# Six layer norms of a two-block transformer kernel: shift by the mean of the first chunks, sum squares while the last chunks come

## The reference

```python
def layer_norm(x, g, b):
    xf = x.astype(jnp.float32)
    mu = jnp.mean(xf, axis=-1, keepdims=True)
    var = jnp.mean(jnp.square(xf - mu), axis=-1, keepdims=True)
    return ((xf - mu) * lax.rsqrt(var + LN_EPS) * g + b).astype(x.dtype)

for l in range(DEPTH):                                   # DEPTH = 2
    h = layer_norm(ALPHA * h + 0.5 * swiglu(h, ffn1_w_up[l], ffn1_w_down[l]), ln_g[l, 0], ln_b[l, 0])
    mix = hybrid_mixer(h, ...)                           # its last product is with w_o
    h = layer_norm(ALPHA * h + mix, ln_g[l, 1], ln_b[l, 1])
    h = layer_norm(ALPHA * h + 0.5 * swiglu(h, ffn2_w_up[l], ffn2_w_down[l]), ln_g[l, 2], ln_b[l, 2])
```

## Time and profile before

| | before |
|---|---|
| median of 3 runs | 2914.3 us (2912.72 to 2917.24) |
| the profiled execution, its own time | 2911.84 us |
| its span in the trace | 2909.9 us |
| TensorE busy | 2790.0 us, 96% of the span |
| VectorE busy | 1999.8 us, 69% |
| ScalarE busy | 1681.8 us, 58% |
| GpSimd busy | 637.7 us, 22% |
| mean granted TensorE clock | 0.979 |

### The profile page before, as it was taken

One profiled execution on the slowest core, in us unless ns is written; L12 is line 12 of the kernel. 1 busy time (PEld: TensorE's weight loads), 2 busy tenths in 40 slices (PEclk: granted clock), 3 DMA queues, 4 the chain that ended last, 5 costly groups with the idle time before them and its releaser, 6 DMA issues.

```text
span 2909.9 us, 67986 instructions
## 1 busy us (share of the span) xinstructions
PE 2790.0 (96%) x27848; PEld 2301.9 (79%) x27848; DVE 1999.8 (69%) x1916; ACT 1681.8 (58%) x1776; POOL 637.7 (22%) x489
## 2 busy tenths in 40 slices
PE   9999989989999899799989999989999999999998
PEld 7877768878877688597878888779788797797884
DVE  4556565555565645566755465768899999999986
ACT  5435655455356454445655445636777777777775
POOL 3304012111031121002012002013242242332432
PEclk9999999999999999899999999989999999999999
DMA  8664357666633566463466754448999999999996
GB/s 231 172 186 134 93 161 198 172 170 178 199 116 106 162 175 175 126 190 121 150 167 190 216 161 134 127 157 308 382 391 378 393 384 379 395 379 382 393 381 235
DMA packets 657500, 665.40 MB, mean 229 GB/s; under 512 B 25302, under 2 KB 513116, under 8 KB 657276
## 3 DMA queue, kind: packets, MB, share of 16 engines
q1 hardware_dynamic: 655696, 659.75, 69.1%
q0 software_dynamic: 704, 0.59, 0.3%
q10 hardware_dynamic: 876, 1.79, 0.2%
HBM read 661.01 MB, written 1.05 MB: 228 GB/s over the span
## 4 chain that ended last, share of the span: by engine, by line
PE 89%; DVE 4%; ACT 2%; issue 2%; DVEq 1%; POOL 0%; DMA 0%; POOLq 0%; ACTq 0%; SPq 0%
PE ps L1793 22%; PE ps L1795 22%; PE ps L1794 22%; PE ps L2414 3%; PE ps L2413 3%; PE ps L2415 3%; PE ps L1834 1%; PE ps L1835 1%; PE ps L1840 1%; PE ps L1934 1%; DVE w_lo L1115 1%; PE ps L2046 1%; PE ps L1940 1%; PE ps L2066 1%; PE ps L2370 1%
## 5 line engine op out<-in xcount | busy, mean ns | idle before, releaser
L1793 PE MATMUL ps<-x_hi,w_hi 128*128 128x128 f16 (+2 forms) x5440 | 1232.6, 250 | 15.0 <-DVE prod L1130 7.3
L1795 PE MATMUL ps<-x_hi,w_lo 128*128 128x128 f16 (+2 forms) x5440 | 1232.3, 250 | 0.0
L1794 PE MATMUL ps<-x_lo,w_hi 128*128 128x128 f16 (+2 forms) x5440 | 1232.1, 250 | 0.0
L1115 DVE SCALAR_TENSOR_TENSOR w_lo<-w,w_hi 128x2048 f16<-128x2048 f32 (+4 forms) x338 | 689.7, 2051 | 323.6 <-ACT w_hi L659 319.4
L659 ACT ACTIVATE w_hi<-w 128x2048 f16<-128x2048 f32 (+4 forms) x338 | 563.8, 1673 | 182.8 <-PE ps L1795 157.9
L1793 PEld LDWEIGHTS ps<-x_hi,w_hi 128*128 128x128 f16 x5440 | 533.9, 98 | 74.0 <-issue 14.6
L1794 PEld LDWEIGHTS ps<-x_lo,w_hi 128*128 128x128 f16 x5440 | 533.9, 98 | 49.4
L1795 PEld LDWEIGHTS ps<-x_hi,w_lo 128*128 128x128 f16 x5440 | 533.7, 98 | 46.2
L1535 DVE SCALAR_TENSOR_TENSOR w_lo<-w,w_hi 128x2048 f16<-128x2048 f32 x224 | 544.8, 2456 | 31.2 <-ACT w_hi L1045 31.2
L1045 ACT ACTIVATE w_hi<-w 128x2048 f16<-128x2048 f32 x224 | 419.1, 1904 | 43.0 <-DMA w<-in_moe_w_down 21.3
L1775 POOL CAST ff<-pb 128x512 f16<-128x512 f32 x56 | 140.2, 2503 | 634.3 <-DVE pb L1616 634.3
(11 more groups left out here) (346 smaller groups left out, 4270.6 us busy)
## 6 DMA issues: line engine op xcount, KB each, us to landing
w<-in_ffn_w_up SPq DMA_DIRECT2D x176, 512.0 KB, 5.1
w<-in_moe_w_gate SPq DMA_DIRECT2D x80, 1024.0 KB, 9.0
w<-in_moe_w_up SPq DMA_DIRECT2D x80, 1024.0 KB, 9.2
w<-in_moe_w_down SPq DMA_DIRECT2D x64, 1024.0 KB, 8.2
w<-in_w_in SPq DMA_DIRECT2D x112, 512.0 KB, 4.7
mix<-in_moe_w_down SPq DMA_DIRECT2D x48, 1024.0 KB, 8.5
w<-in_mix_w_in SPq DMA_DIRECT2D x64, 512.0 KB, 4.9
mix<-in_moe_w_gate SPq DMA_DIRECT2D x32, 1024.0 KB, 9.6
```

Of the source, the lines that this page charges most:

```text
L1115: vec.scalar_tensor_tensor(k.w_lo[:, s, 0:size], k.w32[:, s, 0:size], WS, k.w_hi[:, s, 0:size], ALU.mult, ALU.subtract).then_inc(k.parts_r ...
L1793: pe.matmul(acc, w_hi, x_hi, start=first, stop=False)
L1794: pe.matmul(acc, w_hi, x_lo, start=False, stop=False)
L1795: return pe.matmul(acc, w_lo, x_hi, start=False, stop=last)
```

## The change

All six norms are made over. The constant matrix gets a companion `first_w` whose entries average over the first 6 chunks (down) or the first 4 (`wo`).

- **Shift.** When the first 6 (4) chunks are in, TensorE makes their mean (`shift`), behind unit 12 of a down phase or in the middle of unit 2 of `wo`. VectorE (`center`) subtracts it from these chunks, and prepares the others as `h*WS*ALPHA - shift`, so that the last products are only added to them.
- **Squares.** ScalarE squares the first chunks right away. GpSimd adds the squares up in float32 (`add_squares`: 6 additions for chunks 0 to 6 in a down phase, 3 for chunks 0 to 3 in `wo`), with a drain after each. TensorE takes that sum with one product (in a down phase ahead of unit 15, the last), and the rest of the squares behind the last unit.
- **What is left of the mean.** Only the unsummed chunks are multiplied with `mean_w` (the shifted first ones have sum zero). VectorE copies this rest out of PSUM, squares it, and subtracts the square from the mean of squares. GpSimd takes the rest off all 8 chunks (`take_off`), and VectorE scales each chunk once that is done for it.
- **Order on ScalarE.** The splits of the next phase's units 2 and 3 now stand around the 8 writes of `h`: unit 2 ahead of them, unit 3 behind them. The steps of the next phase that made them leave them out.
- **Clock.** 13 products of `mean_w` with itself (`keep_warm`) behind each norm's last sum; 30 in place of 18 at the start.
- The down phases and `wo` are written out in place of loops, and `wo` on VectorE gets an order by hand.

```diff
-WARM_UP = 18
+WARM_UP = 30
+KEEP_WARM = 13
+EARLY_DOWN, EARLY_WO = 6, 4
+SHIFT_STEP, SQUARES_STEP, SUMS_STEP = 2 * EARLY_DOWN, 2 * EARLY_DOWN + 1, 2 * KC - 2
...
 # ScalarE
+    def early_squares(n, early):
+        for c in range(early):
+            act.wait_ge(k.ln_centered, centered_before(n) + c + 1)
+            square(c)
+    def down_norm(n, phase, q, vec0, between=None):
+        def take(trip, j, g, q):
+            u = trip * SLOTS + j
+            if u == SHIFT_STEP and between is not None:
+                between()
+            if u == SQUARES_STEP:
+                early_squares(n, EARLY_DOWN)
+            if u > SQUARES_STEP:
+                c = EARLY_DOWN + u - SQUARES_STEP - 1
+                if c == KC - 1:
+                    root_ready()
+                act.wait_ge(k.vec_evac, vec0 + phase.base + 2 + c + 1)
+                square(c)
+        over_units_ahead(act, phase, q, split, take, loop=False)
-    def layer_norm(n, b0):
-        root_ready()
-        for c in range(KC):
-            act.wait_ge(k.ln_centered, n * KC + (c + 1))
-            act.activation(k.sq[:, c, :], k.h[:, c, :], ACT.Square).then_inc(k.ln_squared, 1)
-        act.wait_ge(k.ln_var, n + 1)
-        act.activation(k.std[:, 0, :], k.ps[:, 5, 0:T1], ACT.Sqrt, bias=k.eps[:, 0:1]).then_inc(k.ln_std, 1)
+    def layer_norm(n, b0, q, following):
+        act.wait_ge(k.ln_spread, n + 1)
+        act.activation(k.std[:, 0, :], k.tmp[:, 1, :], ACT.Sqrt, bias=k.eps[:, 0:1]).then_inc(k.ln_std, 1)
         for c in range(KC):
             act.wait_ge(k.ln_scaled, n * KC + (c + 1))
             act.activation(k.x_hi[:, c, :], k.sq[:, c, :], ACT.Identity, bias=k.col[:, b0 + c:b0 + c + 1]).then_inc(k.x_hi_ready, 1)
+        split(following + 2, q, UNIT)
         for c in range(KC):
             a = act.activation(k.h[:, c, :], k.sq[:, c, :], ACT.Identity, bias=k.col[:, b0 + c:b0 + c + 1])
         a.then_inc(k.h_ready, 1)
+        split(following + 3, q, UNIT)
...
 # VectorE
-    def add_sum(m):
-        vec.tensor_tensor(k.tmp[:, 2:3, :], k.tmp[:, 2:3, :], k.h[:, bass.ds(m, 1), :], ALU.add).then_inc(k.sum_added, 1)
-        vec.drain()
+    def center(n, early):
+        shift = k.ps[:, 4, 0:T1]
+        vec.wait_ge(k.ln_mean, n + 1)
+        for c in range(early):
+            vec.tensor_tensor(k.h[:, c, :], k.h[:, c, :], shift, ALU.subtract).then_inc(k.ln_centered, 1)
+        for c in range(early, KC):
+            vec.scalar_tensor_tensor(k.h[:, c, :], k.h[:, c, :], WS * ALPHA, shift, ALU.mult, ALU.subtract)
         vec.drain()
+    def down_norm(n, phase, q):
+        def take(trip, j, g, q):
+            u = trip * SLOTS + j
+            if u == SHIFT_STEP:
+                center(n, EARLY_DOWN)
+            if u % 2 == 0:
+                return
+            m, acc = u // 2, k.ps[:, 2 * (j // 2), 0:T1]
+            unit_used(g, q)
+            if m < EARLY_DOWN:
+                vec.scalar_tensor_tensor(k.h[:, m, :], k.h[:, m, :], WS * ALPHA, acc, ALU.mult, ALU.add).then_inc(k.vec_evac, 1)
+                a = add_first(m)
+                if m == EARLY_DOWN - 1:
+                    a.then_inc(k.first_summed, 1)
+            else:
+                vec.tensor_tensor(k.h[:, m, :], k.h[:, m, :], acc, ALU.add).then_inc(k.vec_evac, 1)
+        over_units_ahead(vec, phase, q, split, take, loop=False)
+    def wo_norm(n, q):
+        split(g + 2, q, UNIT)
+        split(g + 3, q, UNIT)
...
+        add_pair(0, True)
+        add_first(1)
+        add_pair(1, True)
+        add_first(2)
+        add_first(3).then_inc(k.first_summed, 1)
+        split(g + 4, q, UNIT)
+        center(n, EARLY_WO)
+        add_pair(2, False)
+        vec.wait_ge(k.wo_half, n // 3 + 1)
+        vec.tensor_tensor(k.h[:, 6, :], k.h[:, 6, :], k.ps[:, 2, 0:T1], ALU.add).then_inc(k.wo_half_out, 1)
+        split(g + 5, q, UNIT)
+        unit_used(g + 3, q)
+        vec.tensor_tensor(k.h[:, 7, :], k.h[:, 7, :], k.ps[:, 3, 0:T1], ALU.add).then_inc(k.vec_evac, 1)
     def layer_norm(n, g0, b0):
-        vec.wait_ge(k.ln_mean, n + 1)
-        for c in range(KC):
-            vec.tensor_tensor(k.h[:, c, :], k.h[:, c, :], k.ps[:, 4, 0:T1], ALU.subtract).then_inc(k.ln_centered, 1)
+        vec.wait_ge(k.ln_rest, n + 1)
+        vec.tensor_copy(k.tmp[:, 0, :], k.ps[:, 4, 0:T1]).then_inc(k.rest_out, 1)
+        vec.drain()
+        vec.tensor_tensor(k.tmp[:, 1, :], k.tmp[:, 0, :], k.tmp[:, 0, :], ALU.mult)
+        vec.drain()
+        vec.wait_ge(k.ln_var, n + 1)
+        vec.tensor_tensor(k.tmp[:, 1, :], k.ps[:, 5, 0:T1], k.tmp[:, 1, :], ALU.subtract).then_inc(k.ln_spread, 1)
         vec.wait_ge(k.ln_std, n + 1)
         vec.reciprocal(k.rstd[:, 0, :], k.std[:, 0, :])
         vec.drain()
         def t(c):
+            vec.wait_ge(k.unshifted, n * KC + (c + 1))
...
 # GpSimd
+    def add_squares(n, last):
+        for c in range(1, last):
+            pool.wait_ge(k.ln_squared, n * KC + (c + 1))
+            pool.tensor_tensor(ss, k.sq[:, 0, :] if c == 1 else ss, k.sq[:, c, :], ALU.add)
+            pool.drain()
+        pool.sem_inc(k.squares_summed, 1)
+    def take_off(n):
+        pool.wait_ge(k.rest_out, n + 1)
+        pool.wait_ge(k.ln_squared, (n + 1) * KC)
+        for c in range(KC):
+            pool.tensor_tensor(k.h[:, c, :], k.h[:, c, :], k.tmp[:, 0, :], ALU.subtract).then_inc(k.unshifted, 1)
+    def down_norm(n):
+        add_squares(n, KC - 1)
+        take_off(n)
...
 # TensorE
+    def down_norm(n, phase, vec0):
+        def behind(u):
+            if u == SHIFT_STEP:
+                shift(n, 0)
+            if u == SUMS_STEP:
+                pe.wait_ge(k.vec_evac, vec0 + phase.base + 2 + KC - 1)
+                add_mean(k.h[:, KC - 2, :], first=True)
+                pe.wait_ge(k.squares_summed, n + 1)
+                add_var(k.prod[:, 0, :], first=True)
+            if u == 2 * KC - 1:
+                pe.wait_ge(k.vec_evac, vec0 + phase.base + 2 + KC)
+                add_mean(k.h[:, KC - 1, :], last=True).then_inc(k.ln_rest, 1)
+                squared(n, KC - 1)
+                add_var(k.sq[:, KC - 1, :], last=True).then_inc(k.ln_var, 1)
+                keep_warm()
+        return behind
```

More of the change, by code:

```diff
@@ L770, in act_program @@
             late = u + AHEAD - win.units
-            split(win.first + u + AHEAD, q, win.size if late < 0 else win.after[late])
+            if u >= 2:
+                split(win.first + u + AHEAD, q, win.size if late < 0 else win.after[late])
             if u == LAT_SQUARED:
@@ L1894, in up, with down @@
         over_units(pe, phase, q, unit)
-    def down(phase, q, vec0, gates, a_hi, a_lo, t, fc):
+    def down(phase, q, vec0, gates, a_hi, a_lo, t, fc, behind=None):
         half = fc // 2
@@ new lines, in add_var, with shift, squared, keep_warm @@
+    def add_var(x, first=False, last=False):
+        return pe.matmul(k.ps[:, 5, 0:T1], k.mean_w[:, :], x, start=first, stop=last)
+    def shift(n, early):
+        pe.wait_ge(k.first_summed, n + 1)
+        pe.matmul(k.ps[:, 4, 0:T1], k.first_w[:, early, :], k.tmp[:, 2, :], start=True, stop=True).then_inc(k.ln_mean, 1)
+    def squared(n, c):
+        pe.wait_ge(k.ln_squared, n * KC + (c + 1))
+    def keep_warm():
+        for _ in range(KEEP_WARM):
+            pe.matmul(k.ps[:, 7, 0:P], k.mean_w[:, :], k.mean_w[:, :], start=True, stop=True)
@@ new lines, in wo_norm @@
+    def wo_norm(n, q, vec0, chunk):
+        phase = S1["wo"]
+        opening(phase, q, k.vec_evac, vec0, k.x_hi, k.x_lo, T1, chunk, P, 256, True)
+        for u in (2, 3):
+            g = phase.first + u
+            weights(g, q)
+            pe.wait_ge(k.vec_evac, vec0 + u + (phase.base + 1))
+            for half in range(2):
+                a = chain(k.ps[:, 2 * (u % 2) + half, 0:T1], g % SLOTS, [(kc * 256 + half * P, P, kc) for kc in range(KC)], k.x_hi, k.x_lo)
+                if (u, half) == (2, 0):
+                    shift(n, 1)
+                if (u, half) == (3, 0):
+                    a.then_inc(k.wo_half, 1)
+                    pe.wait_ge(k.squares_summed, n + 1)
+                    add_var(k.prod[:, 0, :], first=True)
+            a.then_inc(k.unit_done, 1)
+        pe.wait_ge(k.rest_summed, n // 3 + 1)
+        add_mean(k.prod[:, 1, :], first=True)
+        squared(n, 4)
+        add_var(k.sq[:, 4, :])
+        pe.wait_ge(k.vec_evac, vec0 + phase.base + 2 + 4)
+        add_mean(k.h[:, 7, :], last=True).then_inc(k.ln_rest, 1)
+        for c in (5, 6, 7):
+            squared(n, c)
+            a = add_var(k.sq[:, c, :], last=c == 7)
```

150 lines of the change are left out of this document (95 added, 55 removed).

## The result

The changed kernel takes 2924.6 us (median of 7 runs, 2920.7 to 2925.0) against 2914.8 us (7 runs, 2911.3 to 2917.2): a ratio of 1.0032 with a 95% interval of 1.002 to 1.0044. It is slower, by 10 us. The profiled executions have spans of 2923.0 and 2909.9 us, so 13.1 us apart, where the sum had forecast 13.9.

A forecast was written before the change was run, and what follows sets the result against it. TensorE, busy 96% of the span, was taken as the bound. Down norms +21.1 and `wo` -7.2 gave +13.9 us, so 2925.7 on the profiled execution and 2928 us as median; range 2903 to 2937.

The forecast's parts named there:

- The stall: Down norms, ahead of unit 15: TensorE waits 4.0 us for GpSimd's sum of squares, held up by VectorE's splits.
- the sum is in time: Rival, down norms: GpSimd gets more than one addition in between splits; -8.9 us in all, 2905 us; chance 0.22.
- The clock behind it: Unit 15 of the down phases, after the stall: 3.4 us at the lower clock, costing 1.7 us.
- E: End of TensorE's last product ahead of a norm; forecast to come 7.1 us late in down norms.
- The short tail: From E to `x_hi` and H in the norms: gain 3.9 to 1.9 us, taken as 2.9 in down norms.
- H: Moment ScalarE starts writing `h` behind a norm; E + 15.9 before, forecast between E + 12.0 and E + 14.0.
- that rival: Behind all six norms: GpSimd's `take_off` sets the scalings' pace, H moves 2 us more; +26, 2940 us; chance 0.08.
- Behind H: ScalarE's order sets the third unit: H + 7.9 behind norms 0 and 3 (+0.25), H + 9.4 behind 1, 2, 4.
- the clock does not stay up, then nothing changes: Rival, openings behind the norms: sum unchanged, since the opening ends ahead of the third unit's turn; no chance given.
- `wo`: Norms 1 and 4: gain 4.5 to 4.0 us at `x_hi`, taken as 3.6 each at H, -7.2 together.
- The splits in norm 5: Two ScalarE splits around `h` lie on the rms norm's path: 3.8 us of norm 5's +8.0.
- The start: Twelve more warm-up products at the program's start: between +0.2 and -1.7 us, taken as 0.

The follow-up runs named there:

- the kernel with the same products: Changed kernel with TensorE summing all down-norm squares and ScalarE's splits put back, `keep_warm` products kept: 2900.2 us; without those products 2905.2 us.
- Two effects: Against the changed kernel: TensorE sums all down-norm squares, 2910.5 us; ScalarE's unit 3 split and norm 5's splits put back, 2910.0 us; both together 2900.2 us.

## Why the prediction was right, and where it was not

**The stall, right.** Forecast: 4.0 us ahead of unit 15, four times, ended by GpSimd. Measured: 3.65, and 14.5 in all. The order of events was the forecast one too: one addition beside each of the three splits (9.38 us for five; 5.67 when the two long splits are away), the last sum at 204.6 by before's clock; the shift came 2.8 us earlier than there (189.25 against 192.05), and 204.6 - 2.8 = 201.8 stands against the measured 201.52. The rival "the sum is in time" had six times 0.87 us for the additions. An addition that meets no split takes 0.76 us and the next starts 0.14 us behind it, so the price was fair; the rival failed because VectorE's three splits lie in the same stretch. Of these only the short one had been moved there: the long ones began at 196.93 in the kernel before, which is 194.1 by this kernel's clock, and begin at 194.75 here.

**The clock behind it, mis-sized.** I took 1.7 us, from 3.4 us at the lower level. Unit 15 took some 6.1 us in place of 3.82, and the product ahead of it 0.94 in place of 0.46: 2.7 us. The clock was down for longer than behind the 3.7 us of the earlier trace rows. So it was in norm 5 (0.57 over the 8 us from 1210). In norms 2 and 3 the forecast size held (0.72 over the 6 us from 606, 0.68 over the 5.4 from 807.6: 3.4 us at the lower level), and so it did in norm 0 of the changed kernel's second profile (0.72 from 202.3 to 208.3), where the whole norm came out at the forecast +4.45. The size differs between norms and executions; what sets it stays open. E came 5.27 us later in the trace, and the start had gained 2.37, so norm 0 delayed it by 7.6 us, where 7.1 was forecast.

**The short tail, right in form, in the lower half of its range.** The first product at E + 7.4; forecast was E + 6 to 6.7 for the first `x_hi`, which came at 215.51, E + 6.8, just outside. H at E + 13.6, within 12.0 to 14.0, where I had taken 13.0. The run without `take_off` shows both ends: 12.0 without GpSimd, 1.6 us from taking turns. `take_off` doesn't set the pace of the later scalings, which stand at their usual 0.41 us spacing, so that rival is out (eight subtractions in 6.4 us, done at 217.0). The Trainium skill's rule ("SBUF — State Buffer", Who interferes with whom), by which `center` with an operand in PSUM leaves GpSimd free, is borne out: GpSimd's first addition at 191.24 took 0.76 us in the middle of `center`, and `center`'s six subtractions took 2.17 us with it and 2.17 in the kernel whose GpSimd adds nothing there.

**Behind H, right on ScalarE, wrong on the cost of waiting.** Behind norm 0 ScalarE's rows are the forecast ones, and the third unit started at H + 7.64 (7.9 forecast):

```profile
222.31 1.89 ACT L684 ACTIVATE w_hi<-w 128x2048 f16<-128x2048 f32 x1
224.11 3.39 ACT L758 ACTIVATE h<-sq,col 128x272 f32<-128x272 f32 x8
227.41 1.89 ACT L684 ACTIVATE w_hi<-w 128x2048 f16<-128x2048 f32 x1
229.21 1.10 ACT L836 ACTIVATE mix<-ps 128x544 f32<-128x544 f32 x2
```

The step of the prediction that failed is "`keep_warm` I cost at nothing". I had argued that a faster opening only waits longer, and a wait for an engine that is late anyway is free. It is not free when it is long enough for the clock to fall behind it: behind norm 1 the clock stood at 0.53 over 6.13 us, which is 5.8 us at half speed and 2.9 us lost, and behind norm 4 at 0.70 over 5.7, 1.7 us lost. That explains norm 2's miss (4.25 + 2.9 = 7.15, measured 7.2; in the second profile, with no fall behind norm 1, +4.45) and more than half of norm 5's (8.0 + 1.7 = 9.7, measured 10.8; the remaining 1.1 is of the size by which unit 15's clock was mis-sized in that norm, as in norm 0). The rival "the clock does not stay up, then nothing changes" is wrong for the same reason: the kernel without the products is 4 to 5 us faster. The Trainium skill ("TensorE: Matmul & The Clock Gate", HAM oscillation — how this bites in real kernels) describes waits of TensorE that are each followed by a slow stretch; the traces agree for the 11 waits of 3.3 us or more ahead of a third unit, and add that it matters on which side of a wait that costs nothing the slow stretch falls.

**`wo`, right.** -3.3 and -2.5 by the third unit, -3.6 forecast. At the first product behind norm 1 the gain is 4.15 us (3.26 later at `wo`'s opening, 0.89 earlier at 414.50), in the forecast 4.0 to 4.5. Behind norm 4 it is 4.1 by the same working; that the third unit shows only -2.5 comes from the stretch between norm 3's third unit and `wo`'s opening, whose products didn't change and which took 1.0 us longer.

**The splits in norm 5, right.** The rms norm's squares waited 16.4 us in place of 13.07 in the earlier trace rows; the kernel with the two splits behind `h` has 12.84, so 3.6 of the forecast 3.8 us are these splits:

```profile
1240.04 5.94 PE L2154 MATMUL ps<-sq,mean_w 128*128 128x256 f32 x16 [16.43 <-ACT sq L766]
```
```profile
1226.41 5.97 PE L2156 MATMUL ps<-sq,mean_w 128*128 128x256 f32 x16 [12.84 <-ACT sq L768]
```

**The start, wrong.** -2.4 in place of 0, beyond my bound of -1.7. I had written that the products "may keep the clock up a little"; they kept it at 1.00 through the whole opening, and the trace of the kernel before had the 0.83 to cost it from.

**The rest, wrong.** I had assumed that code which isn't touched takes the same time. It took 6.8 us less, and no step of the prediction looked there. Without it, the profile would have shown +19.9.

## What to carry to other kernels

Before you hand an idle engine some work that another must wait for, lay its instructions against the long ones of the engine that it takes turns with, and move those first: the same six additions were late by 3.65 us beside two long splits, and in time without them. An engine's wait for a later one is only free as long as the clock doesn't fall behind it; keeping the clock up ahead of such a wait can lose time (here 4 to 5 us). Once the wait had been shortened, the kernel with the same products had the lower median by 5 us, of which the traces place 3.5. When the end moves little, sum the difference stage by stage before you call a prediction right.

## What the runs showed that I had not expected

- The lower clock moves to behind the wait when the opening is made faster: 11 of 11 waits of 3.3 us or more ahead of a third unit were followed by it, and 2 of 54 of 2.5 us or less.
- Unchanged code behind a changed part takes 1673.2 to 1680.4 us in 13 traces, and one stretch of it either 228.3 or about 232.6 us. A difference of 7 us in a total of 2900 can come from there. It hid 3 of the 8 us of the run without `take_off`.
- Two effects that add up exactly in the stage where they act (12.4 and 13.6 us, together 26.1) came out 3.4 us short in the medians (4.2 by the bare ones), and 1 us short in the traces.
